# Running sums of the log decay in a two-block transformer kernel: one VectorE scan per pair on channel-major logits, in place of TensorE's triangular products

## The reference, cut to what matters

```python
w_log = -softplus(-(w0 + tanh(wd) @ w2)) - 0.5
decay = exp(-exp(w_log))          # = exp(-exp(-0.5) * sigmoid(w0 + tanh(wd) @ w2))
def step(S, inp):
    r_t, w_t, k_t, v_t, a_t, b_t = inp
    sa = einsum('bhvk,bhk->bhv', S, a_t)
    S = (S * w_t[:, :, None, :] + sa[..., None] * b_t[:, :, None, :]
         + v_t[..., None] * k_t[:, :, None, :])
    return S, einsum('bhvk,bhk->bhv', S, r_t)
```

## Time and profile before

| | |
|---|---|
| median of 3 runs | 2886.51 us (2886.08 to 2887.16) |
| profiled execution, its own time | 2888.49 us |
| its span, first to last instruction | 2886.3 us |
| busy: PE, DVE, ACT, POOL | 2851.2, 1729.8, 1222.9, 53.2 us |
| mean granted TensorE clock over the span | 0.997 |
| the eight pairs | about 1396 to 1760 us, some 45 us each |

### The profile page before, as it was taken

The page is one execution under the profiler, slowest core; times in us unless marked ns, Lnnn a source line. Parts: engine busy times, 40 slices in busy tenths (PEclk is TensorE's granted clock), DMA queues, the critical chain, the costliest instruction groups (busy, mean ns, idle before and its releaser), DMA issues.

```text
span 2886.3 us, 53091 instructions
## 1 busy us (share of the span) xinstructions
PE 2851.2 (99%) x22493; PEld 2578.3 (89%) x22493; DVE 1729.8 (60%) x2509; ACT 1222.9 (42%) x1788; POOL 53.2 (2%) x102
## 2 busy tenths in 40 slices
PE   9999999999999999899999999999999999999999
PEld 8999998888888999899888888899998888888887
DVE  6467757656566444754666665666666566665444
ACT  5345544333333343643533343455443333333443
POOL 1000000000000000000000000000000000000000
PEclk9999999999999999999999999999999999999999
DMA  7666455555555555455434335445555555555554
GB/s 245 199 168 168 153 168 167 182 189 189 188 183 181 190 188 181 156 171 168 121 93 113 103 89 160 130 120 180 186 190 178 186 189 189 178 188 172 189 189 146
DMA packets 370325, 485.16 MB, mean 168 GB/s; under 512 B 12359, under 2 KB 181654, under 8 KB 370150
## 3 DMA queue, kind: packets, MB, share of 16 engines
q1 hardware_dynamic: 362752, 471.55, 51.5%
q0 software_dynamic: 4112, 7.88, 0.9%
q10 hardware_dynamic: 3302, 3.39, 0.4%
HBM read 475.76 MB, written 7.01 MB: 167 GB/s over the span
## 4 chain that ended last, share of the span: by engine, by line
PE 91%; DVE 6%; issue 1%; ACT 1%; DMA 1%; DVEq 0%; SPq 0%; ACTq 0%
PE psum L338 20%; PE psum L340 10%; PE psum L344 9%; PE psum L342 9%; PE psum L343 9%; PE psum L550 6%; PE psum L554 5%; PE psum L552 5%; PE psum L717 3%; PE psum L716 3%; PE psum L718 3%; DVE w_lo L328 2%; PE psum L1845 1%; DVE arena L761 1%; PE psum L1831 1%
## 5 line engine op out<-in xcount | busy, mean ns | idle before, releaser
L328 DVE TENSOR_TENSOR w_lo<-w_raw,w_hi 128x1024 fp32r<-128x1024 f32 x728 | 859.1, 1222 | 799.4 <-ACT w_hi L319 799.3
L319 ACT ACTIVATE w_hi<-w_raw 128x1024 fp32r<-128x1024 f32 x728 | 731.3, 1052 | 1162.4 <-PE psum L340 591.1
L338 PE MATMUL psum<-act,w_hi 128*128 128x512 f32 x2816 | 989.5, 394 | 9.1 <-issue 4.5
L340 PE MATMUL psum<-act,w_lo 128*128 128x256 f32 x2816 | 790.6, 281 | 0.0
L342 PE MATMUL psum<-act,w_hi 128*128 128x256 f32 (+3 forms) x2320 | 656.4, 283 | 8.2 <-issue 4.5
L343 PE MATMUL psum<-act,w_hi 128*128 128x256 f32 (+3 forms) x2320 | 656.6, 283 | 0.0
L344 PE MATMUL psum<-act,w_lo 128*128 128x256 f32 (+3 forms) x2320 | 656.4, 283 | 0.0
L338 PEld LDWEIGHTS psum<-act,w_hi 128*128 128x128 f32 x2816 | 529.5, 188 | 137.1 <-DVE w_lo L328 11.8
L340 PEld LDWEIGHTS psum<-act,w_lo 128*128 128x128 f32 x2816 | 530.1, 188 | 0.1
L342 PEld LDWEIGHTS psum<-act,w_hi 128*128 128x128 f32 (+1 forms) x2320 | 438.2, 189 | 12.4 <-issue 7.8
L344 PEld LDWEIGHTS psum<-act,w_lo 128*128 128x128 f32 (+1 forms) x2320 | 438.8, 189 | 0.0
(11 more groups left out here) (399 smaller groups left out, 2071.9 us busy)
## 6 DMA issues: line engine op xcount, KB each, us to landing
w_raw<-w_in SPq DMA_DIRECT2D x128, 1024.0 KB, 5.7
w_raw<-w_down SPq DMA_DIRECT2D x88, 1024.0 KB, 5.0
w_raw<-w_gate_up SPq DMA_DIRECT2D x88, 1024.0 KB, 5.0
w_raw<-w_gate SPq DMA_DIRECT2D x44, 1024.0 KB, 5.2
w_raw<-w_up SPq DMA_DIRECT2D x44, 1024.0 KB, 5.2
w_raw<-w_out SPq DMA_DIRECT2D x16, 1024.0 KB, 5.1
w_raw<-w_o SPq DMA_DIRECT2D x16, 1024.0 KB, 4.9
w_raw<-w_branch_a SPq DMA_DIRECT2D x8, 1024.0 KB, 5.1
```

The source lines that it names most:

```text
L319: nc.scalar.activation(w_hi[:, s % 2, 2 * h:2 * h + 2, 0:wd], w_raw[:, s % RAW, 2 * h:2 * h + 2, 0:wd], ACT.Copy).then_inc(hi_ready, 1)
L328: nc.vector.tensor_tensor(w_lo[:, s % 2, 2 * h:2 * h + 2, 0:wd], w_raw[:, s % RAW, 2 * h:2 * h + 2, 0:wd], w_hi[:, s % 2, 2 * h:2 * h + 2, ...
L338: pe.matmul(dst.rearrange("p (h n) -> p h n", h=2), w1, both_parts, start=first, stop=False, skip_group_check=True)
L340: return pe.matmul(dst[:, 0:n], w0, act_hi[:, k, tok], start=False, stop=last, skip_group_check=True)
```

## The change

The decay logits are now computed channel-major, as the `a` logits are: one product, with the slice of `w2` as the stationary operand and the 272 tokens moving. ACT's tanh writes them into a tile `ld` of 275 columns: one free column ahead of each chunk (16, 128, 128 tokens). DVE makes the sigmoid in one instruction over all 275 columns, sums the first half of each chunk with a minus sign into the free column (two reductions), and makes the running sums by one `tensor_tensor_scan` (state = state * table + ld, where the table `chunk_starts` is 0 at the free columns and 1 elsewhere). Column t of a chunk then holds the sum without token t, column t + 1 the sum with it. The triangular products are gone from TensorE's queue, where `side(2)`, products, `side(2)` become `side(4)`. ACT reads the sums in SBUF and brings in the factor by `scale`; each of the three large exponentials becomes two, one for the 16 tokens and one for the two chunks of 128. The tables of the sums (288 columns) are replaced by `chunk_starts` (288 columns). One memset of `ld` is added ahead of the pairs.

```diff
--- before.py
+++ after.py
@@ -68,15 +68,8 @@
     parts["ident_blocks"] = i == j
     parts["room"] = np.zeros((P, 640))
 
-    def sums(n):
-        s, t = np.arange(n)[:, None], np.arange(n)[None, :]
-        mid = (s <= n // 2 - 1).astype(float)
-        incl, excl = (s <= t) - mid, (s < t) - mid
-        m = np.concatenate([incl, excl], axis=1) * DECAY_SCALE
-        return np.concatenate([m, np.zeros((P - n, m.shape[1]))], axis=0)
-
-    parts["sums"] = sums(P)
-    parts["sums_meta"] = sums(META)
+    parts["chunk_starts"] = np.ones((P, 288))
+    parts["chunk_starts"][:, [0, META + 1, META + P + 2]] = 0
     k = np.arange(TOK)[None, :]
     parts["fox_mask"] = np.where(k <= P + META + p[:, None], 0.0, MASKED)
     sel = np.zeros((P, 46))
@@ -1609,7 +1602,10 @@
         a_t, kf, kkn = place(TOK), place(TOK), place(TOK)
         ar = place(2, TOK)
         einv, bh, kh = place(TOK), place(TOK), place(TOK)
-        ld = place(3, P)
+        RUN = META + 2 * P + 3
+        ld = place(RUN)
+        ld_meta = ld[:, 0:META + 1]
+        ld_chunks = ld[:, META + 1:RUN].rearrange("p (c t) -> p c t", c=2)
         toks = place(4, P)
         tokm = place(3, RHD)
         gm0 = place(2, PAIR)
@@ -1645,7 +1641,7 @@
                    "gram", "s32t", "gm0", "v64", "x64t", "v128", "x128"]
         INV_ACT = ["raw0", "p2", "r1t", "s8", "v16", "s16", "v32", "s32", "x64", "v128", "x128"]
         for j in range(8):
-            rw_dve_steps += [(n, j) for n in ["ld", "a", "t1", "kf", "kkn", "rk", "b", "bh", "kh", "ah", "rh",
+            rw_dve_steps += [(n, j) for n in ["ld", "mid", "run", "a", "t1", "kf", "kkn", "rk", "b", "bh", "kh", "ah", "rh",
                                               "bv"] + INV_DVE
                              + ["x0", "u0", "s0", "sh1", "x1", "u1", "sd", "s1", "sh2", "x2", "u2",
                                 "ys", "yc"]]
@@ -1663,7 +1659,7 @@
                   ("v128", 0), ("v128", 1), ("x128", 0), ("x128", 1)]
         rw_pe_steps += [("logits", 0), ("kkspread", 0)]
         for j in range(8):
-            rw_pe_steps += [(n, j) for n in ["sums", "bonus", "toks", "blocks"] + PE_INV
+            rw_pe_steps += [(n, j) for n in ["bonus", "toks", "blocks"] + PE_INV
                             + ["x0", "u0", "s0", "x1", "u1", "y1s1", "x2", "u2", "y2"]]
             rw_pe_steps += [(n, j + 1) for n in ("logits", "kkspread") if j < 7] + [("yc", j)]
         rw_pe_steps += ["ysum"] + [("out", j) for j in range(8)]
@@ -1761,10 +1757,7 @@
                     pe.wait_ge(*ra.after("tanh"))
                     pe.wait_ge(*rd.after("kkvar"))
                     pe.wait_ge(*rd.after(("z", 25)))
-                for n, t in enumerate(PIECES):
-                    rows = t.stop - t.start
-                    pe.matmul(psum[0:rows, 0, n * P:(n + 1) * P], tw[0:LORA + 1, t], w2s[0:LORA + 1, b],
-                              start=True, stop=True)
+                pe.matmul(psum[:, 0, 0:TOK], w2s[0:LORA + 1, b], tw[0:LORA + 1, :], start=True, stop=True)
                 pe.matmul(psum[:, 1, 0:TOK], a2s[0:LORA, b], z[0:LORA, 25, 1:ZP], start=True, stop=True) \
                     .then_inc(*rp.did(("logits", j)))
                 if j == 0:
@@ -1778,16 +1771,7 @@
 
             front(0)
             for j in range(8):
-                side(2)
-                pe.wait_ge(*rd.after(("ld", j)))
-                for n, t in enumerate(PIECES):
-                    rows = t.stop - t.start
-                    tb = T["sums_meta" if n == 0 else "sums"]
-                    lhs = ld[0:rows, n, :]
-                    pe.matmul(psum[:, 4, t], lhs, tb[0:rows, 0:rows], start=True, stop=True)
-                    mm = pe.matmul(psum[:, 3, t], lhs, tb[0:rows, rows:2 * rows], start=True, stop=True)
-                mm.then_inc(*rp.did(("sums", j)))
-                side(2)
+                side(4)
                 pe.wait_ge(*rd.after(("rk", j)))
                 pe.matmul(psum[:, 0, 0:TOK], T["head_sum"], diff[:, 0], start=True, stop=True) \
                     .then_inc(*rp.did(("bonus", j)))
@@ -2078,20 +2062,25 @@
                 PEA = lambda n: rp.after((n, j))
                 s.wait_ge(*PEA("logits"))
 
-                s.activation(ld[0:META, 0], psum[0:META, 0, 0:P], ACT.Tanh, scale=0.5)
-                s.activation(ld[:, 1:3], psum[:, 0, P:3 * P].rearrange("p (a b) -> p a b", a=2),
+                s.activation(ld_meta[:, 1:], psum[:, 0, 0:META], ACT.Tanh, scale=0.5)
+                s.activation(ld_chunks[:, :, 1:], psum[:, 0, META:TOK].rearrange("p (c t) -> p c t", c=2),
                              ACT.Tanh, scale=0.5).then_inc(*ra.did(("ld", j)))
                 s.activation(a_t, psum[:, 1, 0:TOK], ACT.Tanh, scale=0.5, bias=half_a0[:, j:j + 1]) \
                     .then_inc(*ra.did(("a", j)))
                 side(2)
-                s.wait_ge(*PEA("sums"))
-                s.activation(ar[:, 0], psum[:, 3, 0:TOK], ACT.Exp)
-                s.activation(ar[:, 1], psum[:, 4, 0:TOK], ACT.Exp)
-                s.activation(einv, psum[:, 4, 0:TOK], ACT.Exp, scale=-1.0)
-
-
-                s.activation(to_mid, psum[:, 3, META:META + P + 1:P], ACT.Exp, scale=-1.0)
-                s.activation(from_mid, psum[:, 4, META - 1:META + P:P], ACT.Exp) \
+                s.wait_ge(*rd.after(("run", j)))
+
+                def decay(dst, at, sign):
+                    scale = sign * DECAY_SCALE
+                    s.activation(dst[:, 0:META], ld_meta[:, at:at + META], ACT.Exp, scale=scale)
+                    s.activation(dst[:, META:TOK].rearrange("p (c t) -> p c t", c=2),
+                                 ld_chunks[:, :, at:at + P], ACT.Exp, scale=scale)
+
+                decay(ar[:, 0], 0, 1.0)
+                decay(ar[:, 1], 1, 1.0)
+                decay(einv, 1, -1.0)
+                s.activation(to_mid, ld_chunks[:, :, 0], ACT.Exp, scale=-DECAY_SCALE)
+                s.activation(from_mid, ld[:, META:META + P + 2:P + 1], ACT.Exp, scale=DECAY_SCALE) \
                     .then_inc(*ra.did(("exp", j)))
                 side(4)
                 s.wait_ge(*PEA("toks"))
@@ -2167,6 +2156,7 @@
             v.memset(inv[:, 0:META], 0.0)
             v.memset(gm0, 0.0)
             v.memset(tokm, 0.0)
+            v.memset(ld, 0.0)
             v.memset(raw, 0.0)
             v.memset(inv_t, 0.0)
             v.memset(inv64, 0.0)
@@ -2186,8 +2176,14 @@
                 D_ = lambda n: rd.did((n, j))
                 A_ = lambda n: rd.after((n, j))
                 v.wait_ge(*ra.after(("ld", j)))
-                v.tensor_scalar(ld[0:META, 0], ld[0:META, 0], 0.5, 0.5, ALU.mult, ALU.add)
-                v.tensor_scalar(ld[:, 1:3], ld[:, 1:3], 0.5, 0.5, ALU.mult, ALU.add).then_inc(*D_("ld"))
+                v.tensor_scalar(ld, ld, 0.5, 0.5, ALU.mult, ALU.add).then_inc(*D_("ld"))
+                v.wait_ge(*A_("ld"))
+                v.tensor_reduce(ld[:, 0:1], ld[:, 1:META // 2 + 1], AX, ALU.add, negate=True)
+                v.tensor_reduce(ld_chunks[:, :, 0], ld_chunks[:, :, 1:P // 2 + 1], AX, ALU.add, negate=True) \
+                    .then_inc(*D_("mid"))
+                v.wait_ge(*A_("mid"))
+                v.tensor_tensor_scan(ld, T["chunk_starts"][:, 0:RUN], ld, 0.0, ALU.mult, ALU.add) \
+                    .then_inc(*D_("run"))
                 side(2)
                 v.wait_ge(*ra.after(("a", j)))
                 v.tensor_scalar(a_t, a_t, 0.5, 0.5, ALU.mult, ALU.add).then_inc(*D_("a"))
@@ -2373,7 +2369,7 @@
         fmx_s, fsum_s, frs_s = (small[:, c:c + 8].rearrange("p (a b) -> p a b", a=2)
                                 for c in (32, 40, 48))
         assert at0 <= FOX_AT
-        scan_tab = tab[:, table_at["upper8"][0]:table_at["sums_meta"][1]]
+        scan_tab = tab[:, table_at["upper8"][0]:table_at["chunk_starts"][1]]
         fwt = scan_tab[:, 0:768].rearrange("p (h t) -> p h t", h=2)
         fl2, c_neg = small2[:, 1], small2[:, 1]
```

## The result

| | before | changed |
|---|---|---|
| median, 19 runs each | 2887.16 us | 2891.65 us |
| ratio, 95% interval | | 1.0016 (1.0010 to 1.0022) |
| profiled execution, span | 2886.3 us | 2890.1 us |

One execution of the changed kernel took 10843.51 us at a mean clock of 0.244 and is left out of the ratio.

The account below looks back on a forecast made before the run. VectorE's chain up to `rk` was taken to bound the pairs, so only the logits count: 3.3 − 0.3 = 3.0 us gained, 1.6 lost to one clock fall. Profiled execution 2887.1, median 2885.1 us; range 2880 to 2893.5.

Parts of the forecast that it names:

- the products' 1.45 us would become a stall at `rk`: TensorE ahead of `bonus`: removing the triangular products gains nothing; their 1.45 us a pair become a 1.35 us wait for VectorE.
- where I took 0.68: VectorE's chain ahead of `rk`: the scan takes 0.68 us, bounded by 0.43 below and 1.85 above.
- forecast 6.96: Pair 2: the transposes start 6.96 us after the start of `yc`, against 7.34 before, 0.38 gained.
- I count one such fall, in pair 5: TensorE's clock: one fall to 1.2 GHz behind the gap of 2.6 us in pair 5, 1.6 us lost.
- the 2.07 of the earlier trace: TensorE's record before the change: after a 2.07 us gap the clock fell to 1.2 GHz, costing 1.6 us.
- Gaps of up to 1.7 us occur 23 times: TensorE behind L328: 23 gaps of up to 1.7 us without a clock fall, cited against falls after ordinary 1.35 us gaps.
- saved 0.41: Token-major logits on TensorE: 0.87 us becomes 0.46 with the new product, 0.41 saved a pair, 3.3 us in all.
- the table by pairs: Start of the transposes in each pair: 1.3 us gained, 1.6 lost in pairs 5 and 7, sum −0.3 us.
- the 1.96 of the earlier trace: TensorE behind `rk`: `bonus` and two side steps take 1.96 us before the transposes start.
- −3.0 + 1.6 = −1.4 us: Whole kernel: 3.0 us gained from logits less the pairs' loss, 1.6 lost to one clock fall.

Follow-up runs that it names:

- Experiment 1: Changed kernel with six useless products, shaped like the triangular ones, put back at their old place on TensorE; 2886.66 us, ratio 0.9996 to the kernel before.
- experiment 2: Changed kernel without the scan instruction, so ScalarE reads the sigmoids; 2885.63 us, ratio 0.9995 to the kernel before.
- experiments 4: Changed kernel with VectorE's sigmoid, reductions and scan for the next pair moved ahead of its wait for `yc`; 2879.76 us, ratio 0.9969 to the kernel before.
- 6: Changed kernel with two TensorE side steps moved from behind the block products to ahead of the wait for `rk`; 2882.62 us, 0.9977 to the kernel before.
- 7: Changed kernel with four more ScalarE exponentials in each pair, into an unused place; 2893.45 us, ratio 1.0015 to the kernel before.
- Experiment 3: Changed kernel with a second scan ahead of the first, into an unused place; 2900.66 us, ratio 1.0042 to the kernel before.
- 5: As experiments 4, with the two short forgetting-attention chains on VectorE also moved ahead of the wait for `yc`; 2883.28 us, ratio 0.9974 to the kernel before.
- 10: As experiments 4, with one TensorE side step moved from behind the block products to ahead of the wait for `rk`; 2877.95 us, 0.9968 to the kernel before.
- 8: Kernel before, with only its VectorE sigmoid of `ld` moved ahead of the wait for `yc`; 2887.08 us, ratio 0.9996 to the kernel before.
- 9: As experiments 4, with the six products kept on TensorE behind a wait for `yc`; 2883.70 us, ratio 0.9984 to the kernel before.

## Why the prediction was wrong, step by step

**Right: the mechanism.** The prediction said that the products' 1.45 us would become a stall at `rk`. Its `rk` was at +4.94, and it ended at +4.91; the stall was to be 1.35 us in pair 2 and is 1.35; in pair 5 2.6, and is 2.62; in pair 7 about 2.0, and is 2.14. The scan takes 0.73 us where I took 0.68. By the Trainium skill, "DVE: opcode table, instruction layouts, handler registers and perf-mode slots", section "Datapath and trigger behaviour", where the built-in scan program runs at half throughput, the estimate was 0.72: the trace agrees with it. The reductions take 0.16 and 0.28 us, ScalarE's eight exponentials end at +4.0, the transposes start at +7.05 (forecast 6.96) in pair 2. Experiment 1 fills this wait at a cost of about 1 us, experiments 2, 4 and 6 shorten it and gain, and 7 shows that ScalarE's exponentials don't set the time.

**Wrong: the number of falls of the clock, from "I count one such fall, in pair 5".** This is the step that turned the sign. The profiled execution has three in the pairs. That of pair 7 follows a gap of 2.14 us of the matmuls; the prediction had it at about 2.0, just under the 2.07 of the earlier trace rows, and took that for a boundary. That of pair 4 is not behind a wait for `rk`, but among small products, behind 1.51 us of TensorE's own issue. Two falls more than counted are 3.3 us at 1.65 each (the transposes of pair 5 start 1.64 us later than forecast), most of what is missing.

The boundary had little under it. "Gaps of up to 1.7 us occur 23 times" is true of the longest alone: 22 of these 23 gaps are 0.43 to 0.69 us long and one is 1.75, so they say next to nothing of gaps of 1.3 to 2 us. And at the very place of the earlier trace rows the gap of the changed kernel is shorter, and the clock falls from 1789.43 us on all the same:

```profile
1789.06 0.79 PE L1977 MATMUL psum<-small,tab 16*64 16x256 f32 x4 [1.72 <-DMA arena<-rwkv_g]
...
1789.43:1792.84 3.41, 3.41 (x14) 2.70 (x11) 0.91 (x2) 0.00 (x0) 0.69 (x1) 0.50 0.00 0
```

Experiment 3 shows that long waits for `rk` bring such falls. Where the one in pair 4 comes from is open, but it goes with the change: in pair 4 the longest gap of TensorE's own issue is 1.37 to 2.61 us in all eight profiles without the six products (the changed kernel and experiments 2 to 7 and 10), and at most 0.98 us in the four with them (the kernel before and experiments 1, 8 and 9). A fall of the clock stands at it in five of the eight and in none of the four. Together the longer issue gaps have not grown: those of the weight loads above 0.7 us are 1.05, 1.11 and 0.98 us in the kernel before, 3.1 together, and 1.51, 0.73 and 0.74, 3.0 together, in the changed one. They have moved, and one has grown.

**Off in size: the logits, "saved 0.41".** The new product takes 1479.80 − 1479.24 = 0.56 us, not 0.46, so 0.31 are saved, 2.5 us in all. `bonus` with two side steps behind it was a poor measure of a product that stands alone; why it came out short was not looked into.

**Off in size: the table by pairs, "−0.3".** The transposes start later against `yc` than before by +0.18, −0.29, 0, +0.04, +2.52, −0.16 and +1.65 us in pairs 1 to 7, together 3.9. Taking from it what lies above the forecast in pairs 5 and 7, where the clock was low (9.87 − 8.23 = 1.64, and 8.49 − 7.55 = 0.94), leaves 1.4 us lost, not 0.3. Experiment 1, without a fall in the pairs, has the same chain and 1.6 us by the same count. The forecast took pairs 1 and 4 to be like 3 and 2; they lose 0.18 and 0.04 where it had gains of 0.1 and 0.38. In pair 4 `rk` was at +4.23 before, not +3.89, which no row had shown. `bonus` to transposes takes 2.09 us behind an idle stretch, 0.13 more than the 1.96 of the earlier trace rows.

**The sum again.** Forecast −3.0 + 1.6 = −1.4 us. With two more falls (+3.3), the logits (+0.8) and the table (+1.1) it is +3.8; the spans differ by 3.8. That it fits to a tenth is partly luck: what pair 0 gained and the shifted issue gaps are not in it. Over all executions the mean clocks say the same, 5.2 us lost against the 1.6 counted. The error is that two terms of one mechanism were priced on their own: a stall on TensorE costs its length, and, where the clock falls behind it, also half of the 3.4 us at low clock; for the length from which that happens I had a single gap. As the gain left over was only 3 us, the sign hung on that count.

## What to carry to other kernels

Work taken off the busiest engine is gained only if the next wait of its queue is ready earlier by as much. Compare, from a common point, when the waited-for result is made and when the engine comes to the wait: here 1.19 us of slack stood against 1.45 us of work removed, and the work was moved into that very chain. Put the moved work where its new engine idles (2.0 to 2.7 us ahead of `yc`), and the change turns from 1.0016 to 0.9969. Stream work pulled ahead of the wait does part of it (0.9977). Useless work in the wait gains no time of its own, but it kept the clock up here (0.9977 against 0.9953), and the kernel came out 5 us faster.

When a change adds idle stretches to TensorE, price the clock apart from the stretches, by the mean clock of many executions, and don't draw a boundary from one gap.

## What the runs showed of the hardware

- The scan over 128x275 fp32 takes 0.73 us, against 0.43 for an ordinary two-operand pass over 272 columns.
- After waits for `rk` of 2.2 to 3.5 us (idle time of the weight loads) in the midst of dense work, TensorE's granted clock mostly went to 1.2 GHz for 3.4 us: at 10 of 12 such waits, two each in the changed kernel and experiment 7 and the eight of experiment 3. That costs some 1.65 us each time. Of the 50 shorter waits for `rk` in these profiles one had a fall.
- The length alone doesn't decide it. Gaps of 2.21 and 2.37 us in experiment 3 had no fall. One of 2.09 us had a fall in pair 5 of experiment 2 and none in pair 0 of the changed kernel and of experiments 4 and 5. Ones of 1.92 us (1.72 of the matmuls) behind a DMA, at 1789 us in the changed kernel, and of 1.51 us amid small products had one.
- Executions of the same kernel differ in their mean clock: in those of the changed kernel 0.996 goes with 2889.2 to 2891.7 us, 0.994 with 2894.5 to 2895.4. How many falls an execution has was seen in the profiled ones alone.
